# A separate three-half ring for the modulation weights, a two-place ring for the section weights, and an earlier first refill

## The reference

```
mod = silu(c) @ w_ada + b_ada              # shift, scale, gate for both halves
h   = rms_norm(x, norm_mix_g) * (1 + sc_m) + sh_m
z   = h @ w_in       # sc_x | sc_B | sc_C | u | v | gate_A | gate_B, 1024 each
y_a = sc_b * causal_dwconv3(sc_c * sc_x, conv_w)
v   = layer_norm(gelu(v), ln_v_g)
y_b = gelu(u) * (tril(w_s) @ v per chunk and group + b_s)
x   = x + g_m * ((sigmoid(gate_a) * y_a + sigmoid(gate_b) * y_b) @ w_out)
h   = rms_norm(x, norm_ffn_g) * (1 + sc_f) + sh_f
top 4 of 32 experts per token:  gu = h @ w_gu[e] + b_gu[e];  y = act(gu) @ w_dn[e] + b_dn[e]
x   = x + g_f * (softmax-weighted sum of y);   out = rms_norm(x, final_norm_g)
```

## Time and profile before

| what | value |
| --- | --- |
| runs | 1152.95, 1155.37, 1156.95 us |
| profiled execution | 1153.63 us, span from first to last instruction 1151.8 us |
| busy | PE 957.4, DVE 357.2, ACT 243.4, POOL 8.6 us |
| moved | 467.30 MB, mean 406 GB/s |

### The profile page before, as it was taken

The page is one execution under the profiler, slowest core; times in us unless marked ns, Lnnn a source line. Parts: engine busy times, 40 slices in busy tenths (PEclk is TensorE's granted clock), DMA queues, the critical chain, the costliest instruction groups (busy, mean ns, idle before and its releaser), DMA issues.

```text
span 1151.8 us, 23787 instructions
## 1 busy us (share of the span) xinstructions
PE 957.4 (83%) x9707; PEld 505.7 (44%) x9708; DVE 357.2 (31%) x801; ACT 243.4 (21%) x365; POOL 8.6 (1%) x28
## 2 busy tenths in 40 slices
PE   7989999998986976987888888888876876876784
PEld 5789999743442321433333333443321322331331
DVE  3689796571221111212121121221211211211112
ACT  3435444530110110111111111110100100100112
POOL 0010000000000000000000000000000000000000
PEclk9989999999998998999998999999998998898997
DMA  9999788999999999999999999999999999999996
GB/s 358 377 340 357 293 311 318 412 400 428 427 425 427 426 426 427 426 426 425 425 426 427 427 426 426 427 426 427 426 426 426 427 426 427 427 426 426 427 424 273
DMA packets 62413, 467.30 MB, mean 406 GB/s; under 512 B 5180, under 2 KB 6516, under 8 KB 27572
## 3 DMA queue, kind: packets, MB, share of 16 engines
q1 hardware_dynamic: 62144, 466.65, 98.1%
q10 hardware_dynamic: 244, 0.29, 0.1%
HBM read 465.87 MB, written 1.05 MB: 405 GB/s over the span
## 4 chain that ended last, share of the span: by engine, by line
PE 42%; DMA 40%; SPq 8%; DVE 6%; issue 4%; ACT 1%; PEldq 0%; DVEq 0%; ACTq 0%
PE B L1405 22%; DMA trio<-in_w_down_dram 21%; DMA W<-in_w_down_dram 14%; PE B L1093 10%; SPq L411 4%; PE B L1424 3%; DMA W<-in_w_gate_up_dram 3%; SPq L413 3%; PE B L1414 2%; DVE wl L743 2%; DMA spare<-in_w_ada_dram 2%; PE B L1351 2%; PE B L1357 1%; DMA raw<-in_w_in_dram 1%; DVE spare L793 1%
## 5 line engine op out<-in xcount | busy, mean ns | idle before, releaser
L1405 PE MATMUL B<-W,trio 128*32 128x512 f32 (+1 forms) x4784 | 451.4, 522 | 85.6 <-DMA W<-in_w_gate_up_dram 77.3
L1405 PEld LDWEIGHTS B<-W,trio 128*32 128x32 f32 x4784 | 163.3, 112 | 347.7 <-issue 168.2
L661 ACT ACTIVATE EW<-EW 128x256 f32<-128x256 f32 x46 | 19.2, 416 | 683.1 <-DVE EW L1023 683.1
L1023 DVE TENSOR_SCALAR EW<-B 128x256 f32<-128x256 f32 x46 | 19.5, 425 | 463.9 <-PE B L1405 463.9
L1093 PE MATMUL B<-hh,wh 128*128 128x256 f32 x384 | 110.4, 288 | 4.2 <-DVE wl L743 4.2
L1093 PE MATMUL B<-hl,wh 128*128 128x256 f32 x384 | 109.8, 286 | 0.0
L1093 PE MATMUL B<-hh,wl 128*128 128x256 f32 x384 | 109.7, 286 | 0.0
L1414 PE MATMUL B<-b_gu,trio 128*32 128x512 f32 x368 | 50.4, 616 | 66.6 <-issue 55.2
L743 DVE TENSOR_TENSOR wl<-raw,wh 128x2048 fp32r<-128x2048 f32 (+1 forms) x36 | 73.3, 2074 | 18.2 <-ACT wh L556 17.7
L556 ACT ACTIVATE wh<-raw 128x2048 fp32r<-128x2048 f32 (+1 forms) x36 | 60.2, 1719 | 84.0 <-DMA raw<-in_w_in_dram 53.8
L1093 PEld LDWEIGHTS B<-hh,wh 128*128 128x128 f32 x384 | 74.9, 195 | 4.6 <-issue 4.0
(11 more groups left out here) (245 smaller groups left out, 689.8 us busy)
## 6 DMA issues: line engine op xcount, KB each, us to landing
W<-in_w_gate_up_dram SPq DMA_DIRECT2D x112, 2048.0 KB, 35.2
W<-in_w_down_dram SPq DMA_DIRECT2D x48, 2048.0 KB, 38.4
spare<-in_w_gate_up_dram SPq DMA_DIRECT2D x16, 2048.0 KB, 28.6
trio<-in_w_down_dram SPq DMA_DIRECT2D x15, 2048.0 KB, 41.0
raw<-in_w_in_dram SPq DMA_DIRECT2D x12, 2048.0 KB, 9.5
raw<-in_w_ada_dram SPq DMA_DIRECT2D x9, 2048.0 KB, 9.6
raw<-in_w_in_dram SPq DMA_DIRECT2D x4, 1024.0 KB, 15.7
raw<-in_w_out_dram SPq DMA_DIRECT2D x2, 2048.0 KB, 8.9
```

The lines of the kernel that those rows point to most:

```text
L661: A(sg, gs, ACT.Sigmoid, scale=ALPHA).then_inc(sig_ready, 1)
L1023: V.tensor_scalar(halves(gs), paired(GU[:, 0:QC]), LIMIT, None, ALU.min).then_inc(gmin_ready, 1)
L1405: t = M(o, src[:, k % KQ, CAP * (k // KQ):CAP * (k // KQ) + CAP], w, start=(first and k == 0), stop=(k == KT - 1))
```

## The change

Four things change together.

1. `raw` keeps two places for sections (V 1, then SC_C and so on in turn). The third place and the second half of `spare` become three *half places* of 1 MB. The 2 MB modulation loads of the passes 1 and 2 become sixteen half loads, c = 0 to 15, that go round these three places; `weigh` waits for and frees them one by one. The halves are issued by SP behind the section loads that `HALVES_AFTER` names, half c when half c - 3 has been used.
2. `weigh` moves: (1,0) to h0 SC_C, (1,1) to h0 SC_B, (1,2) to h0 GATE_A, (1,3) to h0 U, (2,0) to h0 GATE_B, (2,1), (2,2), (2,3) to h1 SC_C, SC_B and GATE_A, always in bank 0. `sum_weighed(1)` moves behind the spatial product that follows h0 U, and `sum_weighed(2)` stays behind h1 GATE_A. Some small loads move later in SP's order, and units 0 and 1 are issued ahead of the last output load.
3. `ln_v_g` is no longer spread over 128 partitions (a 512 KB transfer) and multiplied into `HV` (L813, twice); it comes as 4 KB, is transposed with the other small rows, and is applied in the U section by two `scalar_tensor_tensor` in place of one `tensor_tensor` per bank.
4. `FIXED` is 5. The `freed` counts of these five come from an early scan, so the refills of experts 2 and 3 wait for `first_freed` and not for `order_ready`. `wts4` and its transposes move behind the first `hTg`, and `open_sum` moves from ahead of expert 0 to between experts E-2 and E-1. `gs` moves from `EW` to `mod`.

```diff
+    ADA_WEIGHED = {at: (1 + n // 4, n % 4) for n, at in enumerate(WEIGHED_IN)}
+    HALVES_AFTER = {(0, SC_C): (0, 1, 2), (0, GATE_A): (3, 4), (0, GATE_B): (5, 6), (1, SC_C): (7, 8), (1, SC_X): (9, 10),
+                    (1, SC_B): (11, 12), (1, GATE_A): (13, 14), (1, GATE_B): (15,)}
+    ADA_SUMMED = {(0, U_): 1, (1, GATE_A): 2}
+    BIAS_ADDED = {(0, GATE_B): 1, (1, U_): 2}
-        FIXED = 2
+        FIXED = 5
...
             for n, (kind, s, h) in enumerate(units):
-                if n not in ASIDE and place(n) >= RING:
-                    m = next(o for o in range(n) if o not in ASIDE and place(o) == place(n) - RING)
+                m = None if n in ASIDE else tenant_of(n)
+                if n == NU - 1:
+                    sp.wait_ge(ada_summed, NH)
+                    load(0, 0)
+                    load(1, 0)
...
+                if kind == "in" and s != V_:
+                    for c in HALVES_AFTER.get((h, s), ()):
+                        i, q, k = 1 + c // 8, c // 2 % 4, c % 2
+                        if c >= 3:
+                            sp.wait_ge(ada_half, c - 2)
...
+                        sp.dma_start(ada_half_at[c % 3], ada_v[q, :, k, 4 * HALF * i:4 * HALF * (i + 1)]).then_inc(s_ada[c % 3], 16)
...
+            sp.wait_ge(first_freed, 1)
+            for q in range(TURN):
+                next_expert(q, UNITS * q, e=q + TURN)
             sp.wait_ge(order_ready, 2)
-            with sp.Fori(0, TURNS - 1) as i:
+            with sp.Fori(1, TURNS - 1) as i:
...
             split_low(2)
-            weigh(1, 0)
             split_low(3)
...
-            for a in range(TA):
-                step(V.tensor_scalar(HV[:, a, :], HV[:, a, :], stat[:, NMU + a:NMU + a + 1],
-                                     stat[:, VRST + a:VRST + a + 1], ALU.add, ALU.mult))
-                V.tensor_tensor(HV[:, a, :], HV[:, a, :], lng, ALU.mult).then_inc(v_ready, 1)
+            for a in range(TA):
+                V.tensor_scalar(HV[:, a, :], HV[:, a, :], stat[:, NMU + a:NMU + a + 1],
+                                stat[:, VRST + a:VRST + a + 1], ALU.add, ALU.mult).then_inc(v_ready, 1)
...
-                        if b == 0 and n < 3:
-                            weigh(1 + h, n + 1)
-                        if b == 0 and s == GATE_B and h + 1 < NH:
-                            weigh(2 + h, 0)
+                        if b == 0 and (h, s) in ADA_WEIGHED:
+                            weigh(*ADA_WEIGHED[h, s])
...
-                    if s == GATE_A:
-                        sum_weighed(1 + h)
+                    if (h, s) in ADA_SUMMED:
+                        sum_weighed(ADA_SUMMED[h, s])
...
             expert(E - 2, 0, TURNS)
+            n = pe.snap(rnd, min_val=1, max_val=ALL_ROUNDS)
+            pe.wait_ge(spread_out, 2 * NQ * n + NQ)
+            pe.wait_ge(wT_ready, 1)
+            pe.wait_ge(gf_used, NQ + 1)
+            for a in range(TA):
+                for h in range(NH):
+                    open_sum(a, h)
+            pe.wait_ge(opened, NH * TA)
             expert(E - 1, 1, TURNS, split=True)
```

More of the change, by code:

```diff
@@ L61, in hybrid_trunk @@
     SPLITS = 2
+    WEIGHED_IN = [(0, SC_C), (0, SC_B), (0, GATE_A), (0, U_), (0, GATE_B), (1, SC_C), (1, SC_B), (1, GATE_A)]
+    ADA_WEIGHED = {at: (1 + n // 4, n % 4) for n, at in enumerate(WEIGHED_IN)}
+    HALVES_AFTER = {(0, SC_C): (0, 1, 2), (0, GATE_A): (3, 4), (0, GATE_B): (5, 6), (1, SC_C): (7, 8), (1, SC_X): (9, 10),
+                    (1, SC_B): (11, 12), (1, GATE_A): (13, 14), (1, GATE_B): (15,)}
+    ADA_HALVES = 16
+    ADA_SUMMED = {(0, U_): 1, (1, GATE_A): 2}
+    BIAS_ADDED = {(0, GATE_B): 1, (1, U_): 2}
     units = [("ada", 0, q) for q in range(4)] + [("in", V_, h) for h in range(NH)]
@@ L140, in hybrid_trunk @@
         scm = late[:, 7 * P + 2 * E + 2 * KT:7 * P + 2 * E + 3 * KT]
+        lng = late[:, 7 * P + 2 * E + 3 * KT:7 * P + 2 * E + 4 * KT]
         sig = late[:, 8 * P:8 * P + HALF]
@@ L144, in hybrid_trunk @@
         hf = tmp[:, D:3 * D].rearrange("p (k t) -> p k t", t=T)
-        rows = EW[0:7 * KT, HALF:HALF + P]
+        rows = EW[0:8 * KT, HALF:HALF + P]
         row_sum = stat[:, 58:59]
@@ L173, in hybrid_trunk @@
         key, key_turned, ahead, rank_row, hit_id, hit_more = [order_row(i) for i in range(6)]
[L174 removed]
+        id_row, more_row, _, upto, passed, hit_round, round_row = [order_row(6 + i) for i in range(7)]
+        unit_row = mod[:, 0, 15 * E:16 * E]
         rank_col, id_col, more_col, owner, expert_col, place_rank = [stat[:, 51 + i:52 + i] for i in range(6)]
@@ L186, in hybrid_trunk @@
         UNITS = 6
-        PLACE = ("spare", 2, 0, 8, 9, 1, 3, 4, 5, 6, 7, "trio")
+        PLACE = ("spare", 2, 1, 8, 9, 0, 3, 4, 5, 6, 7, "trio")
         TURN = 2
@@ L313, in place, with turn_of, tenant_of @@
         def place(n):
-            return n if n < ASIDE[0] else n - len(ASIDE)
+            if n <= ASIDE[0]:
+                return n
+            return (split_units.index(n) + 1) % 2
+        def turn_of(n):
+            return sum(1 for o in range(n) if o not in ASIDE and place(o) == place(n))
+        def tenant_of(n):
+            return max((o for o in range(n) if o not in ASIDE and place(o) == place(n)), default=None)
+        ada_half_at = [raw[:, 2 * UW:2 * UW + UW // 2], raw[:, 2 * UW + UW // 2:3 * UW], spare[:, UW // 2:UW]]
         def raw_slot(n):
@@ L405, in _ @@
                         sp.dma_start(b_dn[E * i:E * i + E, :], b_down[0][:, h_dn * HALF:(h_dn + 1) * HALF]).then_inc(s_bdn, 16)
[L407 to L412, removed]
-                    sp.dma_start(unit_pair(u), dn_v[e, j - NQ]).then_inc(s_unit[u % SLOTS], 16)
-            assert [place(n) % RING for n in (NU - 3, NU - 2, NU - 1)] == list(PLACE[1:3]) + [PLACE[5]]
-            sp.wait_ge(ada_summed, NH)
-            load(0, 0)
-            sp.wait_ge(split_l, pieces_before[-3])
-            load(1, 0)
+            assert (place(NU - 2), place(NU - 1)) == (PLACE[2], PLACE[5]) and PLACE[1] == RING - 1
             sp.wait_ge(split_l, pieces_before[-2])
@@ L536, in _ @@
             act.dma_start(rows[5 * KT:7 * KT, :], b_ada[0][0:2 * D].rearrange("(k p) -> k p", p=P)).then_inc(s_rows, 16)
+            act.dma_start(rows[7 * KT:8 * KT, :], ln_v_g[0].rearrange("(k p) -> k p", p=P)).then_inc(s_rows, 16)
             act.wait_ge(cols_ready, 1)
@@ L1374, in _ @@
             t.then_inc(wT_done, 1)
-            pe.wait_ge(hg_ready, 1)
-            pe.wait_ge(table_ready, 1)
-            turn(G, hg, hTg_done)
-            pe.wait_ge(wT_ready, 1)
-            pe.wait_ge(gf_used, NQ + 1)
-            for a in range(TA):
-                for h in range(NH):
-                    open_sum(a, h)
+            pe.wait_ge(x_added, 1)
+            for _ in range(NQ):
+                pe.nop().then_inc(spread_out, 1)
             pe.wait_ge(y_zero, 2)
```

116 lines of the change are left out of this document (65 added, 51 removed).

## The result

| | before | changed |
| --- | --- | --- |
| median, us (lowest to highest) | 1155.72 (1152.95 to 1158.61), 7 runs | 1161.52 (1159.89 to 1164.06), 7 runs |
| ratio, 95% interval | 1 | 1.0065 [1.0053, 1.0077] |
| profiled execution, us | 1153.63, span 1151.8 | 1164.06, span 1162.2 |
| busy PE, DVE, ACT, us | 957.4, 357.2, 243.4 | 962.8, 355.0, 243.4 |

What follows compares the result with a forecast made beforehand. Loading the experts' weights bounds the kernel, so its time follows when TensorE ends its sections, plus a fixed string of transfers. Terms -0.3 + 3.1 + 4.6 = +7.4 us gave 1162 us, range 1153.5 to 1166.5.

Steps and rivals of the forecast that it cites:

- terms 1 and 2: First half: sum_weighed(1) waits for VectorE's weighing, -0.3 us net; second half: TensorE idles for weigh(2,3), +3.1 us.
- The start of the stretch: First half: VectorE's work from the normalisation of v at 68.35 us starts +0.6 us later, bounds -0.5 and +1.5.
- The rival on the other side: Both sums: weighings done in time, so TensorE isn't held; -5.6 us, so 1150 us; chance 0.15.
- term 3: Behind both TensorE stops: clock drops to half, 2.3 us lost at each, +4.6 us, bounds 0 and +5.8.
- The prediction's second place: Experts in the earlier trace: after idle 2.08 us, 64 matmuls took 8.45 us instead of 6.87; 1.7 us lost.
- The late load: h1 GATE_A: its load comes later than its split by more than some 4 us cover; 2 to 4 us, 1165; chance 0.08.
- Part 4: Units 0 and 1, early refill, open_sum, five fixed experts, SP's new wait: each priced at 0.
- The opening: Ahead of expert 0: a wait for transposed weights replaces open_sum; TensorE doesn't bound there; 0, bounds -1.1 and +0.5.
- The sign "the same 427 GB/s to the end": Expert weight loading: after the delayed start, transfers stream at the same 427 GB/s to the end.
- The early refill: First refill could go about 1.5 us earlier, but the last first-load is still in flight; 0, bounds -1.0 and 0.
- the five fixed experts and the moved small loads: Experts: five fixed keep the number of rounds, 0, bounds 0 and +1; SP's wait ahead of section loads, 0.

Runs made afterwards that it cites:

- both later, old opening: Changed kernel with both sums over partitions one section later, the experts' opening as before the change, and unit 1 issued earlier: 1149.23 us, ratio 0.9948.
- stops filled, old opening: Changed kernel with warming transposes ahead of the two sums, and wts4, its transposes and open_sum in the old order: 1155.63 us, ratio 1.0006.
- both later, old opening, no early refill: Kernel with both sums later and the old opening, but SP waits for order_ready, not first_freed, ahead of the first refill: 1149.53 us, ratio 0.9961.
- old opening: Changed kernel with wts4, its transposes and open_sum back in their old order; early refill and five fixed experts stay: 1160.09 us, ratio 1.0047.
- both later: Changed kernel with both sums over partitions one section later, pass 2 weighings, some half loads and units 0 and 1 moved along: 1150.67 us, ratio 0.9958.
- open_sum early: Changed kernel with open_sum ahead of expert 0 again; wts4 and its transposes stay late: 1161.83 us, ratio 1.0061.
- stops filled: Changed kernel with 40 and 28 identity transposes ahead of TensorE's waits for weigh(1,3) and weigh(2,3): 1158.80 us, ratio 1.0032.
- one later: Changed kernel with only sum_weighed(2) moved behind h1 U, its bias behind h1 GATE_B, units 0 and 1 behind the last output load: 1158.71 us, ratio 1.0027.

## Why the prediction was right, and where it wasn't

**VectorE holds the sums (terms 1 and 2): right.** Predicted and measured: h0 SC_B at 76.6 and 75.82 us; TensorE at the first sum at 113.8 and 118.12 - 4.49 = 113.63; weigh(1,3) done at 118.95 and 117.92; GATE_B at 120.1 and 120.05. That last agreement hides two errors: the sum began 1 us earlier and took 1 us longer, for the clock. The start of the stretch, where I had added 0.6 us for a later load, was 68.23 for 68.35. At the second sum the wait was predicted at 3.1 us and was 3.23, with everything 1.75 us later, since the slow sections stand in front of it. Moving the sums, with VectorE's total work unchanged, removed both stops, and moving the second alone removed the second; so it is the place of the sum, not a transfer. The rival on the other side asked for the same condition. Its 1150 us looks like the 1150.67 measured once that was made true, but as a difference to the kernel before it priced -5.6 us where -4.0 was measured (0.42% by the ratio, 4.9 us): 5.3 us are there when unit 11 is issued, and the opening, which the rival had at nothing too, takes a part back. With the old opening it is 5.5 us by the medians (1154.71 and 1149.23).

**The clock (term 3): right in kind, and its size varies from run to run.** Predicted 4.6 us, bounds 0 and 5.8. The profiled execution lost (1.93 - 0.99) + (36.68 - 34.56) = 3.1 us behind the first stop, and (1.94 - 0.99) + (2.01 - 1.09) + (12.59 - 11.51) = 3.0 behind the second, 6.0 in all and over the bound. By the ratios it is 1.0065 - 1.0032 = 0.0033 (changed kernel against the one with transposes) and 1.0047 - 1.0006 = 0.0041 (the same with the old opening), 3.8 to 4.7 us. Both can be true: the second stop cost the clock in two of the three profiled executions that have it and no transposes, and nothing in the third. The Trainium skill (TensorE: Matmul & The Clock Gate, section Why this matters for your kernels) warns of idle gaps of about this length between bursts of matmuls; the trace agrees for the stops of 4.49 us, all four of them, while for 3.23 us it went either way. Shorter gaps cost it here too. The prediction's second place, 2.08 us in the earlier trace rows, is shorter than what the page warns of, so it doesn't side with the rule as I wrote; and in the router the clock was lost behind an idle 0.78 us in two executions and not in the other eight, for 1.2 and 2.8 us. This loss wasn't in the sum at all, and it moves single profiled executions by as much as the terms in question.

**The late load: it didn't happen.** The split of h1 GATE_A began with 2.60 us of waiting for ScalarE, but the chain has ScalarE's piece at 156.81 directly behind TensorE's 36.68 us: it waited for the product that used its buffer, and its weights were there.

**Part 4 (the rest, cost nothing or nearly): the step that was wrong.** Two of its zeros were not zero, with opposite signs.

The opening was costed at 0 with bounds -1.1 and +0.5, by the sentence that TensorE is not what bounds there. Measured: 1.0065 to 1.0047 with the stops cold, and 1.0032 to 1.0006 with them filled, so 0.0018 and 0.0026, 2 to 3 us, outside the bounds. The intervals of the first pair overlap, those of the second don't. TensorE bounds there through the release of one buffer: it waits 1.39 us for the late `wts4` and 1.94 us with nothing queued, loses the clock, and frees the place of unit 12 a quarter of a microsecond after unit 11 has landed. The sign "the same 427 GB/s to the end" failed with it: 348 and 141 GB/s in two windows of 4 us. The slices of the earlier trace rows, 28.8 us each, are too wide to show this; in windows of 4 us the kernel before has its own dent, 387 and 401.

The early refill was costed at 0, since unit 11 was still in flight when the refill was issued. In flight was not enough. The lead is the landing of unit 11 minus the issue of the refill, both counted from unit 11's issue; beside it stands the transfer time missing against 426 GB/s in the two 4 us windows of the hand-over:

| kernel | refill issued | unit 11 lands | lead, us | missing, us |
| --- | --- | --- | --- | --- |
| both later, old opening | 8.93 | 14.3 | 5.4 | 0.0 |
| stops filled, old opening | 9.05 | 13.9 | 4.9 | 0.0 |
| both later, old opening, no early refill | 9.87 | 13.9 | 4.0 | 0.8 |
| before | 10.23 | 13.8 | 3.6 | 0.6 |
| old opening | 8.94 | 11.9 | 3.0 | 0.6 |
| both later | 13.33 | 15.6 | 2.3 | 1.4 |
| open_sum early | 11.97 | 13.4 | 1.4 | 2.0 |
| stops filled | 12.65 | 13.4 | 0.8 | 2.6 |
| one later | 12.50 | 12.9 | 0.4 | 3.4 |
| changed | 13.45 | 13.2 | -0.3 | 3.4 |

Each row is one profiled execution; the names stand for the experiments above ("stops filled" has the transposes, "later" and "one later" the moved sums). A refill queued some 5 us ahead of the landing leaves no gap, one at the landing 3.4 us, and the kernel before, at 3.6 us with 0.6 missing, already had one. The early count did bring the 1.5 us that I had read out of the release (the refill is issued 1.76 us into the 64 matmuls in place of 3.26), and there they were worth some 0.6 to 0.8 us of transfer time, within my bounds of -1.0 and 0; in device time this isn't settled, since the one kernel that takes the early refill back differs by 0.3 us (medians) to 0.0013 (ratios). In the kernel with filled stops it gives 0.6 us back of the 2.3 us that the stops cost. That leaves 1.7 us, the upper end of the interval measured there (0.7 us, -0.3 to +1.7); why the middle of it is 1 us lower stays open.

So the sum, +7.4 us, came close (5.8 by the medians, 7.5 by the ratio), and in part by luck: the waits were worth less in time than in the chain (+0.7 us net of the early refill, bounds -0.3 and +1.7, where I had +2.8), the clock had about the forecast size, and 2 to 3 us came from an opening that I had put at nothing. Two errors of some 2 us each had opposite signs. That clock and opening are separate losses is supported by each having nearly the same price with and without the other: 0.0033 and 0.0041, 0.0018 and 0.0026. The differences are smaller than the intervals, so an overlap of 1 us between them is not excluded. That the five fixed experts and the moved small loads cost nothing is supported only in so far as nothing is left to explain; they were not run alone.

## What to carry to other kernels

An instruction that needs another engine's result belongs at the place in its queue where that result will be ready: with two sums one section later, and the loads and weighings that go with them, the kernel was 11 us faster (1161.52 and 1150.67). Price a stop with the clock behind it, and if a stop can't be moved, fill it with transposes whose result nobody reads. "TensorE doesn't bound there" has to be asked of each buffer that TensorE frees: a transfer in flight covers the next one only if that is queued well before the landing (some 5 us in this kernel, with 2 MB each).

## What the hardware showed that I had not expected

- A stop of 3.23 us on TensorE, the same in three kernels with the same instructions around it, was followed by half the clock in two executions and full clock in the third (1.94 and 1.06 us for the same eight matmuls).
- An idle 0.78 us in the router was enough in two of ten profiled executions: the clock stood at 0.50 behind it until 242 us, at 1.00 in the eight others.
- The refill in the changed kernel met an idle queue: issued at 261.11 us, no data in the window of 261 to 262, 246 GB/s in the next. 2 MB took 7.8 us to land, of which 4.9 are the size at 427 GB/s.

```profile
261.00:262.00 1.00, 1.00 (x16) 0.27 (x11) 0.00 (x0) 0.00 (x0) 0.00 (x0) 1.00 0.00 0
262.00:263.00 1.00, 1.00 (x12) 0.27 (x8) 0.00 (x0) 0.00 (x0) 0.00 (x0) 1.00 1.24 246
```

- What stays open: why TensorE stands 1.94 us with nothing to wait for ahead of expert 0 when no matmul is queued there, and 0.39 to 0.57 us where `open_sum` on early weights precedes it. In the other three kernels with nothing queued there it is 1.66 to 2.01 us. That the registers of the round are set there is my guess; the trace doesn't show it.
